# Stage seams by token tile, counts first in the router, and one sum per tile at the end, in a two-model fp32 kernel

## The reference

```python
# first model: layer 0 a gated delta net, layer 1 a differential attention, each with a dense feed-forward
x = layernorm(ALPHA * x + gt1 * mixer(x * (1 + sc1) + sh1))
x = layernorm(ALPHA * x + gt2 * swiglu(x * (1 + sc2) + sh2))
# second model: layer 0 (RWKV-7 beside latent attention), dense feed-forward; layer 1 (two attentions), experts
h = h + concat(a(rmsnorm(h)), b(rmsnorm(h))) @ w_out
h = h + swiglu(rmsnorm(h))            # layer 0, hidden width 2816
h = h + moe(rmsnorm(h))               # layer 1: 8 experts of width 3584, top 2 by router logits
return rmsnorm(h)
```

## Time and profile before

| | us |
|---|---|
| median of 3 runs | 3343.61 (3340.81 to 3343.63) |
| the profiled execution, its own time | 3341.53 |
| its span in the profile | 3339.7 |
| PE busy | 3157.6 (95%) |
| DVE busy | 798.3 (24%) |
| ACT busy | 488.7 (15%) |
| DMA queue 1, share of 16 engines | 53.2% |
| mean granted TensorE clock | 0.971 |

### The profile page before, as it was taken

The page is one execution under the profiler, slowest core; times in us unless marked ns, Lnnn a source line. Parts: engine busy times, 40 slices in busy tenths (PEclk is TensorE's granted clock), DMA queues, the critical chain, the costliest instruction groups (busy, mean ns, idle before and its releaser), DMA issues.

```text
span 3339.7 us, 40074 instructions
## 1 busy us (share of the span) xinstructions
PE 3157.6 (95%) x16840; PEld 2233.4 (67%) x16840; DVE 798.3 (24%) x1687; ACT 488.7 (15%) x1112; POOL 108.4 (3%) x119
## 2 busy tenths in 40 slices
PE   7999998999999998899698899998999999999997
PEld 3566666477777676577486477685676777767764
DVE  1566666310200233100255200032100100100101
ACT  1332332010000123100221200122000000000001
POOL 0111121000000000000000000000000000000000
PEclk8999999999999999999799899998999999999999
DMA  6333127264444522344301244440999999999995
GB/s 226 114 99 135 45 78 289 90 201 154 150 137 155 162 64 63 111 154 151 96 17 38 89 151 151 127 114 14 358 382 378 351 380 378 334 377 382 331 379 215
DMA packets 417713, 636.27 MB, mean 191 GB/s; under 512 B 11158, under 2 KB 304637, under 8 KB 410245
## 3 DMA queue, kind: packets, MB, share of 16 engines
q1 hardware_dynamic: 412301, 612.49, 53.2%
q0 software_dynamic: 5248, 21.46, 2.0%
HBM read 632.70 MB, written 1.20 MB: 190 GB/s over the span
## 4 chain that ended last, share of the span: by engine, by line
PE 86%; DVE 4%; SPq 2%; issue 2%; ACT 2%; DMA 1%; DVEq 1%; PEld 1%; PEldq 1%; ACTq 0%; POOL 0%
PE PS L790 18%; PE PS L3493 11%; PE PS L798 9%; PE PS L1143 6%; PE PS L3514 5%; PE PS L3500 5%; PE PS L3540 3%; PE PS L3013 2%; PE PS L596 2%; PE PS L1704 2%; PE PS L1700 1%; PE PS L1957 1%; PE PS L1280 1%; PE PS L1295 1%; PE PS L287 1%
## 5 line engine op out<-in xcount | busy, mean ns | idle before, releaser
L817 DVE TENSOR_TENSOR scratch<-scratch,PS 128x128 f32<-128x128 f32 (+1 forms) x200 | 69.3, 347 | 1466.1 <-ACT scratch L807 1465.6
L790 PE MATMUL PS<-XT,WF 128*128 128x256 f32 x1472 | 324.7, 381 | 1.8 <-ACT XT L541 1.8
L790 PEld LDWEIGHTS PS<-XT,WF 128*128 128x128 f32 x1472 | 281.1, 191 | 51.6 <-issue 12.0
L790 PE MATMUL PS<-XT,WO 128*128 128x256 f32 x1344 | 296.0, 379 | 0.0
L790 PEld LDWEIGHTS PS<-XT,WO 128*128 128x128 f32 x1344 | 255.3, 190 | 49.3 <-issue 16.3
L807 ACT ACTIVATE scratch<-PS 128x128 f32<-128x128 f32 (+1 forms) x200 | 64.9, 325 | 1445.0 <-PE PS L790 822.7
L1143 PE MATMUL PS<-XT,WH 128*128 128x512 f32 x512 | 240.7, 597 | 0.0
L3493 PEld LDWEIGHTS PS<-scratch,WO 128*128 128x128 f32 x1792 | 208.6, 192 | 24.9 <-issue 24.6
L3493 PEld LDWEIGHTS PS<-scratch,WF 128*128 128x128 f32 x1792 | 202.4, 192 | 21.4 <-issue 17.8
L3493 PE MATMUL PS<-scratch,WO 128*128 128x128 f32 x1792 | 209.1, 275 | 0.0
L3493 PE MATMUL PS<-scratch,WF 128*128 128x128 f32 x1792 | 207.2, 276 | 1.2 <-ACT scratch L3637 1.2
(11 more groups left out here) (547 smaller groups left out, 3640.2 us busy)
## 6 DMA issues: line engine op xcount, KB each, us to landing
XT<-in_moe_wg SPq DMA_DIRECT2D x56, 1024.0 KB, 10.9
scratch<-in_moe_wu SPq DMA_DIRECT2D x56, 1024.0 KB, 14.1
OT<-in_moe_wd SPq DMA_DIRECT2D x56, 1024.0 KB, 14.1
WO<-in_ada_w SPq DMA_DIRECT2D x36, 1024.0 KB, 7.3
WF<-in_moe_wg SPq DMA_DIRECT2D x28, 1024.0 KB, 15.2
WF<-in_moe_wu SPq DMA_DIRECT2D x28, 1024.0 KB, 17.0
WF<-in_moe_wd SPq DMA_DIRECT2D x28, 1024.0 KB, 12.0
WO<-in_moe_wg SPq DMA_DIRECT2D x28, 1024.0 KB, 11.3
```

What stands on the lines that cost most here:

```text
L790: mm = nc.tensor.matmul(k.PS[:, 4 + f, w * n:(w + 1) * n], slot.gu[:, w, kb, f * P:(f + 1) * P], rhs(kb), start=kb == 0, stop=kb == KB - 1)
L817: k.nc.vector.tensor_tensor(hid[:, f, :], sg[:, f, :], k.PS[:, 4 + f, n:2 * n], ALU.mult).then_inc(*slots[s].dve.done(f"h{f}"))
```

## The change

- The closing `zero_sum` of the four dense feed-forwards goes; the last downs run tile by tile (both f of tile 0, then both f of tile 1), a "sum" fires for each tile, and the slot's "down" semaphores fire behind a PE drain.
- The turning of the tokens goes by tile. `flip_tensor` writes tile 0 to banks 6 and 7 and tile 1 to banks 0 and 1. In seam A it is a transpose; in B to E it is a matmul of X against a diagonal matrix that holds the tokens' 1/rms (`k.dg`, made by VectorE from the identity, L666 goes), so that scaling and turning are one product. VectorE copies tile 0 out (in B to E), ScalarE tile 1 (both in A).
- In A and C the first ups of the next feed-forward run by tile: products of 128 columns, tile 0's before tile 1 is turned.
- In C and E tile 0 is turned between the two halves of tile 1's output product.
- Seam B: the statistics of both tiles come before either finish, and ScalarE applies mean and 1/std (one 128x1024 activation per tile) in place of L633.
- Router: the logits are made by tile; the counts have a semaphore of their own and a bank of their own, and VectorE sorts by load before it waits for the places. Its loads on the POOL queue wait for tile 0's output product and no longer for the RMS norm; the forget gates' loads (seam D) wait for the output product of round 2, one stage earlier.
- Seam F: each tile's two scatter kinds are added up in PSUM (tile 0 in banks 6 and 7, tile 1 in banks 4 and 5), with one VectorE sum per tile. The gain is multiplied before the RMS value is known; the norm, the two stores (one per tile) and their waits stand ahead of the conditional section on ACT and DVE, and SP passes that section before it waits for the result.

```diff
+def flip_tensor(k, pe, rnd, tile, scaled):
+    for kb in range(KB):
+        out = k.PS[:, FLIP_BANKS[tile] + kb // 4, kb % 4 * P:kb % 4 * P + P]
+        x = k.X[:, tile, kb * P:(kb + 1) * P]
+        if scaled:
+            mm = k.nc.tensor.matmul(out, x, k.dg[:, tile, :], start=True, stop=True)
+        else:
+            mm = k.nc.tensor.transpose(out, x, mat(k, C_ID))
...
+def flip_scalar(k, act, rnd, tile, scale, shift=None):
...
+        a = act.activation(k.XT[:, kb, TCOL[tile]], k.PS[:, FLIP_BANKS[tile] + kb // 4, kb % 4 * P:kb % 4 * P + P],
+                           ACT.Identity, scale=scale(kb), bias=shift(kb) if shift else 0.0)
...
+def flip_vector(k, dve, rnd, col):
+    for g in range(2):
+        dve.wait_ge(*k.flip_pe.at(f"t0{'ab'[g]}", rnd))
+        gain = k.vecs[:, 1, col + 4 * g:col + 4 * g + 4].unsqueeze(2).to_broadcast([P, 4, P])
+        i = k.nc.vector.tensor_tensor(k.XT[:, 4 * g:4 * g + 4, TCOL[0]], tiles_of(k, FLIP_BANKS[0] + g), gain, ALU.mult)
...
+def res_diagonal_vector(k, dve, rnd, tile):
     dve.wait_ge(*k.res_act.at("rstd", rnd))
...
+    k.nc.vector.tensor_scalar(k.dg[:, tile, :], mat(k, C_ID), rstd_col(k, tile), None, ALU.mult
+                              ).then_inc(*k.dg_dve.done("d"))
...
+def downs_by_tile_tensor(k, pe, slot, rnd):
+    pe.wait_ge(slot.dn_in, (rnd + 1) * 16)
+    for tile in range(2):
+        for f in range(2):
+            if tile == 0:
+                pe.wait_ge(*slot.dve.at(f"h{f}", rnd))
+            for half in range(2):
+                mm = k.nc.tensor.matmul(k.PS[:, 2 * tile + half, :], k.hid[:, f, tile * P:(tile + 1) * P],
+                                        slot.dn[:, f, half * 512:(half + 1) * 512], start=False, stop=f == 1)
+        if tile == 0:
+            mm.then_inc(*k.acc_pe.done("sum"))
+    mm.then_inc(*k.acc_pe.done("sum"))
+    pe.drain().then_inc(*slot.pe.both("down0", "down1"))
...
+        for n, (f, tile) in enumerate(((0, 0), (1, 0), (0, 1), (1, 1))):
+            if n == flip_at:
+                flip()
+            if n == 2:
+                pe.wait_ge(*k.flip_act.at("x", FLIPPED[m]))
+            ups_by_tile_tensor(k, pe, slot, f, tile)
...
-    turn_tensor(k, pe, slots, LAST, dense_rounds(m, TURNS), rhs, L, k.hid, range(4))
-    zero_sum(k, False, range(4)).then_inc(*k.acc_pe.done("sum"))
+    last = dense_rounds(m, TURNS)
+    turn_tensor(k, pe, slots, LAST[0:2], last, rhs, L, k.hid, range(4))
+    downs_by_tile_tensor(k, pe, slots[0], last[0])
...
+    dve.wait_ge(*k.rt_pe.at("counts"))
+    stt(k.load, k.PS[:, 5, 16:24], float(EXPERTS), k.slot_iota[:, 0:EXPERTS], ALU.mult, ALU.subtract)
+    dve.drain()
+    nc.vector.max(k.loads_down, k.load)
     tt(k.gt[:, :, 1:2], k.gt[:, :, 1:2], k.gt[:, :, 0:1], ALU.mult)
     dve.drain()
...
+    nc.vector.max_index(k.order.bitcast(U32), k.loads_down, k.load)
...
+    dve.drain().then_inc(*k.rt_dve.done("order"))
     tt(k.route[:, 1, :, 0:EXPERTS], k.eq, k.eq2, ALU.add)
...
+    dve.wait_ge(*k.rt_pe.at("places"))
...
+def last_scatter_tensor(k, pe):
...
+    for tile in range(2):
+        bank = (6, 4)[tile]
+        for kind in range(2):
+            if kind and not tile:
+                pe.wait_ge(*k.sums_dve.at("y1", pair))
+            for half in range(2):
+                mm = k.nc.tensor.matmul(k.PS[:, bank + half, :], k.gatedt[:, kind, tile * P:(tile + 1) * P],
+                                        k.ye[:, kind, half * 512:(half + 1) * 512], start=kind == 0, stop=kind == 1)
...
+    for tile in range(2):
+        dve.wait_ge(*k.sums_pe.at(("sc01", "sc11")[tile], pair))
+        tokens_added(k, tile, (6, 4)[tile]).then_inc(*k.sums_dve.both(*(("x00", "x01"), ("x10", "x11"))[tile]))
+        if tile == 0:
+            gained_vector(k, dve, 0)
+    finished_vector(k, dve, 0, k.res_act.at("rstd", 8))
+    gained_vector(k, dve, 1)
+    finished_vector(k, dve, 1, k.res_act.at("rstd", 9))
```

More of the change, by code:

```diff
@@ L587, in out_tensor, with out_tile_tensor @@
         if tile in tiles:
-            out_tile_tensor(k, pe, tile)
+            out_tile_tensor(k, pe, tile, between if tile else None)
         elif rnd:
             pe.drain().then_inc(*k.out_pe.done(f"y{tile}"))
-def out_tile_tensor(k, pe, tile):
+def out_tile_tensor(k, pe, tile, between=None):
     for half in range(2):
+        if half and between:
+            between()
         for kb in range(KB):
@@ L3598, in moe_tensor @@
             duo_step_tensor(k, pe, pair, turn)
-    for kind in range(2):
-        for tile in range(2):
-            duo_scatter_tensor(k, pe, EXPERT_PAIRS - 1, kind, tile)
+    last_scatter_tensor(k, pe)
+def last_scatter_tensor(k, pe):
+    pair = EXPERT_PAIRS - 1
+    pe.wait_ge(*k.sums_dve.at("y0", pair))
+    pe.wait_ge(*k.duo_act.at("tr1", pair))
+    for tile in range(2):
[6 more added lines that the diff above has]
+                                        k.ye[:, kind, half * 512:(half + 1) * 512], start=kind == 0, stop=kind == 1)
+        mm.then_inc(*k.sums_pe.both(*(("sc00", "sc01"), ("sc10", "sc11"))[tile]))
 def more_tensor(k, pe):
@@ L3792, in moe_vector, with gained_vector, finished_vector, again_vector @@
             duo_step_vector(k, dve, pair, turn)
-    for kind in range(2):
-        for tile in range(2):
-            duo_scatter_vector(k, dve, EXPERT_PAIRS - 1, kind, tile)
+    pair = EXPERT_PAIRS - 1
+    for tile in range(2):
[6 more added lines that the diff above has]
+    finished_vector(k, dve, 1, k.res_act.at("rstd", 9))
+def gained_vector(k, dve, tile):
+    dve.drain()
+    k.nc.vector.tensor_tensor(view(k, D * (1 + tile), D), k.X[:, tile, :], k.WH[:, 0, :], ALU.mult)
+def finished_vector(k, dve, tile, ready):
+    out = view(k, D * (1 + tile), D)
+    dve.wait_ge(*ready)
+    dve.drain()
+    k.nc.vector.tensor_scalar(out, out, rstd_col(k, tile), None, ALU.mult).then_inc(*k.fin_dve.done("o"))
+def again_vector(k, dve):
+    for tile in range(2):
+        gained_vector(k, dve, tile)
+        finished_vector(k, dve, tile, k.again_act.at("rstd", tile))
+def again_scalar(k, act):
+    roots_table(act)
+    for tile in range(2):
+        res_scalar(k, act, tile, k.sc_dve.at("x1", EXPERTS - 1), k.again_act)
 def scatter_vector(k, dve, e, tile):
@@ L4110, in vector_program @@
         more_vector(k, dve)
-    dve.drain()
-    for tile in range(2):
-        res_vector(k, dve, 8 + tile, tile, None, k.WH[:, 0, :])
+        again_vector(k, dve)
 def program(nc, t, out):
```

261 lines of the change are left out of this document (160 added, 101 removed).

## The result

The changed kernel takes **3302.64 us** (median of 4 runs, 3301.95 to 3303.86) where the kernel before takes 3343.62 (4 runs, 3340.81 to 3345.17): a ratio of 0.9881, with a 95% interval of 0.9868 to 0.9893, so 41.0 us less. The forecast was 3301, with 3293 to 3313 as its range. The profiled execution took 3301.95 us, its span is 3300.1, and 39.6 us shorter than that of before.

The account below looks back on a forecast made before the run. TensorE held 86% of the chain; the gain was sought in its stops between stages while VectorE and ScalarE make norms. Eight terms summed to 42.3 us: 3299.2 from the profiled execution, 3301.3 from the median, forecast 3301, range 3293 to 3313.

Parts of the forecast that it names:

- the feed-forwards: Feed-forwards 0 and 1: dropping the closing zero products (0.88 us) gains 0.7 us behind 0 and 0.9 behind 1.
- Seam F: Last expert accumulation to final store: two of four sums and 3.05 us at the conditional section go; gain 11.0 us.
- Seam B: Feed-forward 2's last ups to RWKV stage: turning 8.0 us earlier plus 1.6 of clock loss back; gain 9.6, between 8.0 and 14.
- Seam C: Output product to feed-forward 3's ups: tile 0's ups cover tile 1's norm, so nothing waits; gain 5.5 us.
- Seam A: Output product to feed-forward 2's ups: tile 0 turned at once, its ups covering tile 1's layernorm; gain 5.2 us.
- rival 1: Clock falls inside the new seams, 2.3 us more each in A, C and D; gain 34, 3310 us; chance 0.17.
- Seam D: Downs to forget gates: tile 0's sum and norm lie beside tile 1's downs; gain 5.8 us.
- Seam E: Output product to expert start: logits 2.9 us earlier, sort 1.0 more, first load 3.9 earlier; TensorE gains 3.6.
- Rival 2: Expert weights don't follow the earlier start, so 3.6 us are lost: 3305 us; chance 0.07.
- Rival 3: Experts become bound by weight supply and slower; at 340 GB/s the kernel ends at 3368 us; chance 0.03.
- Rival 4: Small overlaps (copies, drains, branch) fail across the seams, costing 5.8 us: 3307 us; chance 0.10.
- The clock and transposes: Transposes count as work for TensorE's clock, so no cold start was charged behind seam A's transposes, against the skill's rule.

Follow-up runs that it names:

- f_scatters: Changed kernel with the last pair's four scatter steps and four sums back, rest of the kernel's end as changed: 3309.55 us, ratio 0.9902.
- cond_inside: Changed kernel plus one untaken conditional section on VectorE, holding only a drain, between the last sums and tile 0's final scaling: 3303.73 us, ratio 0.9886.
- ln_by_tile: Changed kernel with the layernorm before the RWKV stage finished tile by tile and ScalarE's pass back on VectorE: 3307.38 us, ratio 0.9897.
- fill_a: Changed kernel plus ten unused fp32 products in each of three pauses, behind feed-forward 1 and both turnings before feed-forward 2's ups: 3303.3 us, ratio 0.9885.
- fill_all: Changed kernel with the edits of fill_a, fill_e and gates_behind together: 3299.5 us, ratio 0.9872.
- gates_behind: Changed kernel with the forget gates' 8-column products behind the pairs' first 256-column products, and their sums behind the values: 3300.37 us, ratio 0.9875.
- late_loads: Changed kernel with SP's expert loads held until 'ranked' instead of 'order', about 3 us later: 3308.94 us, ratio 0.9898.
- fill_e: Changed kernel plus 36 unused products in the four TensorE pauses around the router (4, 5, 9 and 18): 3302.2 us, ratio 0.988.
- flip_plain: Changed kernel with VectorE scaling the tokens and TensorE turning them by plain transposes, not diagonal products, in seams B to E: 3303.04 us, ratio 0.9886.
- ups_whole: Changed kernel with the first ups of feed-forwards 2 and 3 whole again, 256 columns, both tiles turned before: 3313.25 us, ratio 0.9914.

## Why the prediction was right, step by step

**The size.** The forecast of 42.3 us stands against 39.6 in the span and 41.0 in the medians. Like with like, the working gave 3299.2 us for the profiled execution, and it took 3301.95. It is not right in each term, and part of the match is luck. The stretches that the forecast counts gave 36.9 us, not 42.3; another 2.7 came from stretches whose code is unchanged (1.05 + 1.46 + 0.19), and 2.2 of seam C's from the product ahead of it. Seams B and C gave more than forecast, A, D, E and the feed-forwards less.

**Seam F (11.0, measured 10.8).** The working was right: two sums of 1.22, scatters without a wait, the last pass over 11.2 us behind the experts instead of 22.2. f_scatters puts 6.1 of it on the scatters; I took the 3.05 us at the section for the section's own price, and cond_inside shows that a section around one drain costs nothing. What the 3.05 were stays open.

**Seam B (9.6, measured 10.97).** Here I chose half of the 2.6 us that the clock cost before; all of it came (7.15 against 9.67), though 0.55 were given back soon after. The turning cost 5.73 for both tiles, not 3.7 each: the clock came back before its end, and I had it at half clock throughout (7.4). Interleaving the tiles, with ScalarE's pass in it, is worth 2 us (ln_by_tile). How much the downs by tile, with a sum for each, give of the rest has no run of its own.

**Seam C (5.5, measured 7.19).** The seam itself gave 5.0; 0.8 were lost to the diagonal's 1.11 us. The other 2.2 came from the output product ahead of it, whose first tile ran warm (13.81 us against 16.02, from its first product to tile 1's first). No term of the forecast has them.

**Seam A (5.2, measured 3.28).** This is rival 1 in one seam of four: the clock was at 0.5 within tile 0's ups, at a cost of 1.6 us, and fill_a and fill_all, with the pauses filled, don't have it. I had priced such a fall at 2.3. I had charged nothing, from the rows that showed the clock rising in seam A after transposes; that row tells of a rise, and says nothing of a fall in the pause ahead of the ups. Besides, ScalarE's eight copies took 2.91 us here, not 2.64.

**Seam D (5.8, measured 2.55).** The step that failed is the one not made. I followed the seam to the start of the forget gates, found 5.8, and it was 5.83; I didn't ask what clock these 8-column products would leave behind. They took 5.77 us instead of 3.98 and the next group 9.93; gates_behind gave 2.9 us back.

**Seam E (3.6, measured 2.1).** The seam's own gain was larger than forecast, 4.4 to 4.6: logits 3.2 earlier (2.9 forecast) and the sort 1.3 (1.0 forecast). But the output product ahead of it began at half clock, and its first tile took 2.3 us longer than before (16.10 against 13.81). The logits' 3.2 hold the turning by tile and the router's loads, which in the chain of before stood from 2321.93 to 2325.95; no run has them apart. And the reason I gave for 3.6 was wrong in kind: I let TensorE's gather decide alone, and the load's issue decides as much. Both moved by the same amount in this change, so the number hid it; late_loads and fill_e tell them apart.

**Rival 2** (the weights don't follow) didn't happen: the first load moved by 28.81 us, and the gather by 28.82. **Rival 3** (bound by supply and slower) had half of it right: the experts' start does hang on the supply, but from first load to last zeros they became no longer, to 0.01 us. **Rival 4** (small overlaps) happened in small: the closing zeros' 0.88 us went in feed-forward 0, but the start of the next group won only 0.59 of it (the drain cost about 0.27, priced at 0.2), that group took 0.1 longer, and 0.5 were left of 0.7; behind feed-forward 1 the 0.9 were gone by way of the clock (5.41 against 3.72 us).

**The clock and transposes.** I gave two readings: the row, by which transposes bring the clock back, and the rule of the Trainium skill ("TensorE: Matmul & The Clock Gate", Part 4) that full clock doesn't engage for them. flip_plain decides it: only transposes ran from 1623.42, and the clock stood at 1.0 from 1627. The rule does not hold for these fp32 transposes.

## What to carry to other kernels

A seam ends where the clock is back, not where the first product starts: follow the granted clock for some groups beyond each pause that is moved. Look where narrow products stand: here 32 records of 8 columns cost 2.9 us more directly behind a seam than behind the next 256-column group. Where weights stream through slots at the full rate, find out whether the end hangs on the first load or on the first product: take the time from each to the end in kernels where the two differ, and add up TensorE's waits for loads, which bound what earlier loads alone can win (0.3 us here). The gain from splitting the ups by tile was here the idle time filled plus part of a cold start avoided. And before a stage's gain or loss is put down to an edit, look at the same stage in another execution of the same code: the clock alone moved it by 1.2 us.

## What the runs showed of the hardware that I had not expected

- The time from the first expert load to the end of the experts is the same to 0.1 us in six kernels (971.72 to 971.84), and within 0.7 in all fourteen.
- TensorE's clock fell during work: with 8-column products from 2135.35 to 2138.82 and no pause since 2128.20, it went from 1.0 to 0.5 within 2138 to 2140 (gates_behind); in the kernel before, near the end of the same products, at 2160.
- The clock rose with transposes alone ahead of it: 0.54 in 1626 to 1627, 1.0 after (flip_plain).
- The low clock does not lie in the same place in each kernel. Stages whose code is the same differed by 1 to 2.5 us: the output product of round 1 took 29.2 us in twelve kernels and 30.4 in two (fill_a and ln_by_tile), also between kernels that are the same up to there, and the first tile of that of round 3 took 13.81 us (before, ups_whole) or 15.5 to 16.1 (all others) behind the same small products. What sets this I couldn't tell.
- An untaken conditional section around one drain cost nothing on VectorE (cond_inside); behind the section around a whole program there were 3.05 us.
- The first 600 us, with the same instructions, ended at times up to 6 us apart (the output product behind them began between 605.27 and 611.25 us).
